# Second MLP in pairs of column chunks, with seven products of blocks in place of eight in some units

## Reference

```python
h2 = _rms_norm(x, norm2_g)
x = x + (jax.nn.silu(h2 @ w_gate) * (h2 @ w_up)) @ w_down   # w_gate, w_up: 2048 x 5632; w_down: 5632 x 2048
```

## Time and profile before

| | us |
|---|---|
| median of 3 runs | 2493.56 (2493.5 to 2493.63) |
| the profiled execution, its own time | 2493.6 |
| its span, first to last instruction | 2491.9 |
| TensorE busy in it | 2482.4 (100%) |
| VectorE busy | 1379.8 (55%) |
| ScalarE busy | 1120.3 (45%) |

### The profile page before, as it was taken

How to read it: one execution, slowest core, us unless ns; L and a number is a source line. 1 busy time by engine, 2 the same in 40 slices (tenths; PEclk the granted TensorE clock), 3 DMA queues, 4 the chain that set the end, 5 groups by cost and what they waited for, 6 DMA issues and landing times.

```text
span 2491.9 us, 28047 instructions
## 1 busy us (share of the span) xinstructions
PE 2482.4 (100%) x11885; PEld 2076.6 (83%) x11885; DVE 1379.8 (55%) x1129; ACT 1120.3 (45%) x1100; POOL 116.6 (5%) x95
## 2 busy tenths in 40 slices
PE   9999999999999999999999999999999999999999
PEld 8888888888888888888888888788888888888887
DVE  5675455454655555545555558876544444444444
ACT  5545533434444434334334457874533333333332
POOL 0410010010100000000000010000200000000000
PEclk9999999999999999999999999999999999999999
DMA  7555465666656565565555555444555665565554
GB/s 249 170 185 179 159 196 193 194 194 192 231 186 203 191 198 186 190 198 186 189 192 193 186 186 185 137 157 164 184 188 186 196 192 186 186 200 188 187 189 148
DMA packets 242731, 467.12 MB, mean 187 GB/s; under 512 B 11248, under 2 KB 22016, under 8 KB 242222
## 3 DMA queue, kind: packets, MB, share of 16 engines
q1 hardware_dynamic: 241054, 460.08, 56.9%
q10 hardware_dynamic: 1552, 5.25, 0.5%
HBM read 463.20 MB, written 2.10 MB: 187 GB/s over the span
## 4 chain that ended last, share of the span: by engine, by line
PE 96%; DVE 2%; ACT 1%; issue 1%; POOL 0%; DVEq 0%; ACTq 0%; POOLq 0%
PE acc L409 26%; PE acc L400 26%; PE acc L402 26%; PE acc L429 5%; PE acc L435 2%; PE tp L429 2%; PE sd L429 2%; PE sd L435 1%; PE tp L435 1%; PE tp L455 1%; PE sd L1338 1%; DVE wlo L385 1%; PE tp L1356 0%; PE sd L1347 0%; ACT whi L380 0%
## 5 line engine op out<-in xcount | busy, mean ns | idle before, releaser
L385 DVE TENSOR_TENSOR wlo<-raw,whi 128x2048 fp32r<-128x2048 f32 (+1 forms) x440 | 1014.6, 2307 | 957.8 <-ACT whi L380 957.2
L380 ACT ACTIVATE whi<-raw 128x2048 fp32r<-128x2048 f32 (+1 forms) x440 | 832.2, 1893 | 1067.5 <-PE acc L409 919.5
L400 PE MATMUL acc<-whi,opA_hi 128*128 128x512 f32 x1888 | 740.7, 392 | 0.1
L402 PE MATMUL acc<-whi,opA_lo 128*128 128x512 f32 x1888 | 735.1, 389 | 0.0
L409 PE MATMUL acc<-wlo,opA_hi 128*128 128x512 f32 x1888 | 469.2, 390 | 0.2 <-DVE wlo L385 0.2
L400 PE MATMUL acc<-whi,opB 128*128 128x512 f32 (+1 forms) x1088 | 422.3, 389 | 1.5 <-ACT whi L380 1.5
L402 PE MATMUL acc<-whi,opB 128*128 128x512 f32 (+1 forms) x1088 | 419.1, 386 | 0.0
L400 PEld LDWEIGHTS acc<-whi,opA_hi 128*128 128x128 f32 x1888 | 354.4, 188 | 74.0 <-issue 0.9
L402 PEld LDWEIGHTS acc<-whi,opA_lo 128*128 128x128 f32 x1888 | 354.6, 188 | 72.6
L409 PEld LDWEIGHTS acc<-wlo,opA_hi 128*128 128x128 f32 x1888 | 353.0, 188 | 73.4 <-DVE wlo L385 0.8
L409 PE MATMUL acc<-wlo,opB 128*128 128x512 f32 (+1 forms) x1088 | 266.4, 387 | 0.1
(11 more groups left out here) (308 smaller groups left out, 1297.8 us busy)
## 6 DMA issues: line engine op xcount, KB each, us to landing
raw<-in_w_in SPq DMA_DIRECT2D x116, 1024.0 KB, 5.5
raw<-in_w_mlp_up SPq DMA_DIRECT2D x64, 1024.0 KB, 5.3
raw<-in_w_mlp_down SPq DMA_DIRECT2D x64, 1024.0 KB, 5.0
raw<-in_w_gate SPq DMA_DIRECT2D x44, 1024.0 KB, 5.2
raw<-in_w_up SPq DMA_DIRECT2D x44, 1024.0 KB, 5.1
raw<-in_w_down SPq DMA_DIRECT2D x44, 1024.0 KB, 5.0
raw<-in_w_out SPq DMA_DIRECT2D x32, 1024.0 KB, 5.0
raw<-in_w_branch SPq DMA_DIRECT2D x16, 1024.0 KB, 5.0
```

The lines of the kernel that those rows point to most:

```text
L380: eng.activation(whi[:, j % SPL, k, 0:cols], raw[:, j, k, 0:cols], ACT.Copy).then_inc(hi_split, share(k))
L385: eng.tensor_tensor(wlo[:, j % SPL, k, 0:cols], raw[:, j, k, 0:cols], whi[:, j % SPL, k, 0:cols].bitcast(F32), ALU.subtract).then_inc(lo_s ...
L400: eng.matmul(acc[:, pair, m, 0:cols], hi[:, kt + i, m * P:(m + 1) * P], whi[:, s, i, 0:cols], start=first and i == 0, stop=False)
L402: eng.matmul(acc[:, pair, m, 0:cols], lo[:, kt + i, m * P:(m + 1) * P], whi[:, s, i, 0:cols], start=False, stop=False)
```

## The change

**Pairs.** A run now takes two column chunks at once and all four banks of `acc`. A gate pair is the gate and the up chunk of the same hidden channels: 8 units, each 2 channel tiles of both (`b` = 0 gate, `b` = 1 up). A down pair is two column chunks of down: 6 units in the first part, 8 in the others. The 132 units stay, in 11 gate pairs and 6 down pairs (gate x3, down x2, gate x4, down x2, gate x4, down x2). The load of a unit is two DMAs in place of one.

**Units of seven.** In units 3 and 5 of a pair (only 5 in the first gate pair, 3 and then 1 and 3 in the two down pairs of the first part) the 2 by 2 blocks (two token tiles, two channel tiles, two column chunks) are multiplied by seven products of blocks in place of eight, in Winograd's form of Strassen's algorithm: 21 matmuls in place of 24. That makes 21 such units in gate pairs and 11 in down pairs, 32 of the 132. Three products are summed straight into `acc`, the other four into `sd` and `tp`. VectorE makes four sums of weight blocks per unit (`t_sum`), ScalarE and VectorE split seven blocks of 512 columns in place of four (`seven_high`, `seven_low`). The sums of the activations' blocks are made four times (`operand_sums`): at unit 4 of the first gate pair, and at unit 6 of the last gate pair of each part. The four extra sums are put together behind the last unit of a pair (`combine`, with a copy `q_sum` by ScalarE) and added in as the banks are read.

**The pair's end.** The first and the last unit of a pair go bank by bank (6 matmuls each). All four banks are taken up again by the next pair, so TensorE waits for each bank before its first product in it (`bank_free`): for the SiLU in `acc[:, 0]` behind a gate pair, which itself waits for VectorE's add into the bank, and for VectorE's read elsewhere. VectorE reads the banks (`finish`) behind the split of the next pair's first unit.

```diff
+PAIR_UNITS = KT // 2
+GATE_SEVEN, DOWN_SEVEN = (3, 5), (3, 5)
...
+        PAIRS = []
+        unit, chunks2, seven2 = G_PAIR0 * UN, 0, 0
+        for part, size in enumerate((CH2_FIRST, CH2_LOOP, CH2_LOOP)):
+            for c in range(size):
+                PAIRS.append(Pair(len(PAIRS), "gate", unit, PAIR_UNITS, GATE_SEVEN if PAIRS else GATE_SEVEN[1:], 0,
+                                  GATE_SEVEN[0], (part, c), chunks2))
+                unit += PAIR_UNITS
...
+            for n in range(2):
+                seven = DOWN_SEVEN if part else (1, 3) if n else (3,)
+                PAIRS.append(Pair(len(PAIRS), "down", unit, size * CT // 2, seven, 1, DOWN_SEVEN[0] if part else 1,
+                                  (part, n), chunks2))
+                unit += size * CT // 2
...
+        A_SUMS = {(0, 4): 0}
+        for q in PAIRS:
+            if q.kind == "gate" and PAIRS[q.n + 1].kind == "down":
+                A_SUMS[q.n, 6] = 1
...
+            for p in PAIRS:
...
+                for v in range(p.units):
...
+                    sp.wait_ge(lo_split, (u - RAW + 1) * HV)
+                    to = raw[:, u % RAW].rearrange("p (a b) c -> p a b c", a=2)
+                    for b in range(2):
+                        if p.kind == "gate":
+                            src = (w_gate2, w_up2)[b][:, 2 * v:2 * v + 2, chunk(first + n)]
+                        else:
+                            src = w_dn2[:, first * CT + 2 * v:first * CT + 2 * v + 2, chunk(2 * n + b)]
+                        sp.dma_start(to[:, :, b, :], src).then_inc(landed[u % RAW], 16)
...
+            def seven_high(p, v):
...
+                if last_seven(p, v):
+                    act.wait_ge(units_used, last_seven(p, v))
+                act.activation(seven_hi[:, 0, :], raw[:, u % RAW, 0, :], ACT.Copy)
+                act.activation(seven_hi[:, 1:3, :], raw[:, u % RAW, 2:4, :], ACT.Copy).then_inc(hi_split, 1)
+                act.wait_ge(t_made, 3 * n + 1)
+                act.activation(seven_hi[:, 3:5, :], t_sum[:, 0:2, :], ACT.Copy)
+                act.wait_ge(t_made, 3 * n + 3)
+                act.activation(seven_hi[:, 5:7, :], t_sum[:, 2:4, :], ACT.Copy).then_inc(hi_split, 1)
+            def silu_gates(p):
...
+                act.wait_ge(hidden2, p.gates * MT)
+                for m in range(MT):
+                    act.wait_ge(bank_read, 4 * p.n + m + 1)
+                    act.activation(silu_gate[:, m, :], acc[:, 0, m, :], ACT.Silu, scale=rstd[:, m:m + 1]).then_inc(silu_in, 1)
+            for p in PAIRS:
+                for v in range(p.units):
+                    if v in p.seven:
+                        seven_high(p, v)
+                    else:
+                        hi_unit(act, (p.unit + v) // UN, (p.unit + v) % UN)
...
+                    if v == 0 and p.n and PAIRS[p.n - 1].kind == "gate":
+                        silu_gates(PAIRS[p.n - 1])
...
+                    if (p.n, v) in A_SUMS:
...
+                        act.wait_ge(a_made, n + 1)
+                        act.activation(a_hi[k][:, :, :, :], a_sum[:, :, :, :], ACT.Copy).then_inc(a_high, 1)
+                    if v == p.units - 1:
+                        act.wait_ge(units_used, p.unit + p.seven[-1] + 1)
...
+                        act.activation(q_sum[:, :], sd[:, 0, :], ACT.Copy).then_inc(q_copied, 1)
...
+            def bank_free(p, b, m):
+                if p.n == 0:
+                    pe.wait_ge(read_dve, readers_before(R_PAIR0 - 1 + b, "D") * MT)
+                elif PAIRS[p.n - 1].kind == "gate" and b == 0:
+                    pe.wait_ge(silu_in, PAIRS[p.n - 1].gates * MT + m + 1)
+                else:
+                    pe.wait_ge(bank_read, 4 * (p.n - 1) + 2 * b + m + 1)
+            def plain_products(p, v, hi, lo):
...
+                s, first, last = u % SPL, v == 0, v == p.units - 1
+                pe.wait_ge(hi_split, (u + 1) * HV)
+                def high(b, m, a):
...
+                    pe.matmul(acc[:, b, m, :], hi[:, 2 * v + a, rows], whi[:, s, 2 * a + b, :], start=first and a == 0, stop=False)
+                    pe.matmul(acc[:, b, m, :], lo[:, 2 * v + a, rows], whi[:, s, 2 * a + b, :], start=False, stop=False)
+                def low(b, m, a):
...
+                                     start=False, stop=last and a == 1)
+                banks = [(b, m) for b in range(2) for m in range(MT)]
+                if first or last:
+                    for b, m in banks:
+                        if first:
+                            bank_free(p, b, m)
+                        for a in range(2):
+                            high(b, m, a)
+                        pe.wait_ge(lo_split, (u + 1) * HV)
+                        for a in range(2):
+                            mm = low(b, m, a)
+                        if last and (b, m) != banks[-1]:
+                            mm.then_inc(bank_done, 1)
+                else:
+                    for a in range(2):
+                        for b, m in banks:
+                            high(b, m, a)
+                    pe.wait_ge(lo_split, (u + 1) * HV)
+                    for a in range(2):
+                        for b, m in banks:
+                            mm = low(b, m, a)
+                mm.then_inc(units_used, 1)
+            def seven_products(p, v, hi, lo):
...
+                k1, k2, up, down = 2 * v, 2 * v + 1, slice(0, P), slice(P, T)
+                sums = lambda i: (a_hi[p.op][:, i, x, :], a_lo[p.op][:, i, x, :])
+                own = [(sd[:, 0, :], (hi[:, k1, up], lo[:, k1, up]), 0, True),
+                       (acc[:, 0, 0, :], (hi[:, k2, up], lo[:, k2, up]), 1, False),
+                       (acc[:, 1, 0, :], sums(0), 2, False)]
+                made = [(sd[:, 1, :], sums(1), 3, True), (tp[:, 1, :], sums(2), 4, True), (tp[:, 0, :], sums(3), 5, True),
+                        (acc[:, 0, 1, :], (hi[:, k2, down], lo[:, k2, down]), 6, False)]
+                if first:
...
+                        pe.wait_ge(combined, p.combined)
+                        pe.wait_ge(q_copied, p.n)
...
+                    pe.wait_ge(a_low, sums_made(p))
+                for done, products in ((1, own), (2, made)):
+                    pe.wait_ge(hi_split, u * HV + done)
+                    for bank, (a_h, a_l), i, alone in products:
+                        pe.matmul(bank, a_h, seven_hi[:, i, :], start=alone and first, stop=False)
+                        pe.matmul(bank, a_l, seven_hi[:, i, :], start=False, stop=False)
+                    pe.wait_ge(lo_split, u * HV + done)
+                    for bank, (a_h, a_l), i, alone in products:
+                        mm = pe.matmul(bank, a_h, seven_lo[:, i, :], start=False, stop=alone and last)
+                mm.then_inc(units_used, 1)
+            for p in PAIRS:
+                hi, lo = (opB_hi, opB_lo) if p.op == 0 else (opA_hi, opA_lo)
+                for v in range(p.units):
...
+                    (seven_products if v in p.seven else plain_products)(p, v, hi, lo)
...
+                    if v == 0 and p.n and PAIRS[p.n - 1].kind == "gate":
+                        pe.wait_ge(hidden2, p.turned * MT)
+                        turn(pe, lambda m, b: stage[:, m, b * P:(b + 1) * P], T_HID2 + (p.turned - 1) * MT)
...
+            def seven_low(p, v):
...
+                if last_seven(p, v):
+                    dve.wait_ge(lo_split, last_seven(p, v) * HV)
+                dve.wait_ge(a_low, sums_made(p))
+                dve.tensor_tensor(t_sum[:, 0, :], w[:, 0, :], w[:, 1, :], ALU.add)
+                dve.tensor_tensor(t_sum[:, 1, :], w[:, 1, :], w[:, 3, :], ALU.add).then_inc(t_made, 1)
+                dve.wait_ge(t_made, 3 * n + 1)
+                dve.tensor_tensor(t_sum[:, 2, :], t_sum[:, 0, :], w[:, 3, :], ALU.add).then_inc(t_made, 1)
+                dve.wait_ge(t_made, 3 * n + 2)
+                dve.tensor_tensor(t_sum[:, 3, :], t_sum[:, 2, :], w[:, 2, :], ALU.add).then_inc(t_made, 1)
+                if last_seven(p, v):
+                    dve.wait_ge(units_used, last_seven(p, v))
+                dve.wait_ge(hi_split, u * HV + 1)
+                dve.tensor_tensor(seven_lo[:, 0, :], w[:, 0, :], seven_hi[:, 0, :].bitcast(F32), ALU.subtract)
+                dve.tensor_tensor(seven_lo[:, 1:3, :], w[:, 2:4, :], seven_hi[:, 1:3, :].bitcast(F32),
+                                  ALU.subtract).then_inc(lo_split, 1)
...
+                dve.tensor_tensor(seven_lo[:, 3:7, :], t_sum[:, :, :], seven_hi[:, 3:7, :].bitcast(F32),
+                                  ALU.subtract).then_inc(lo_split, 1)
+            def operand_sums(k, n, p):
...
+                own.done(dve.tensor_tensor(a_full[:, :, :, :], of(hi), of(lo), ALU.add))
...
+                own.mark(dve.tensor_tensor(a_sum[:, 1, :, :], a21, a22, ALU.subtract))
+                own.done(dve.tensor_tensor(a_sum[:, 2, :, :], a21, a11, ALU.subtract))
+                own.done(dve.tensor_tensor(a_sum[:, 3, :, :], a22, a_sum[:, 2, :, :], ALU.subtract))
```

(97 more changed lines are left out.)

198 lines of the change are left out of this document (79 added, 119 removed).

## The result

| | before | changed kernel |
|---|---|---|
| median, us | 2493.5 (7 runs, 2493.24 to 2493.63) | 2501.67 (7 runs, 2500.33 to 2503.89) |
| ratio | | 1.0033, 95% interval 1.0023 to 1.0042 |
| profiled execution: own time, span | 2493.6, 2491.9 | 2502.18, 2500.5 |

The changed kernel is 8.2 us slower, 0.33%. The forecast was 4.6 us slower, 2498.2; the time lies in the range, and the sign is the one that I gave the greater chance. The change itself is 1.8 times the one forecast: it is a small difference of two large sums.

A forecast was written before the change was run, and what follows sets the result against it. TensorE, busy throughout the second MLP, was taken to bound the kernel. 27.0 us of new waits against 22.4 saved made it 4.6 us slower, 2493.6 + 4.6 = 2498.2 us, range 2490 to 2509.

The forecast's parts named there:

- the sign: Whole kernel: slower was given 0.48, same 0.36, faster 0.16.
- The two sums: Second MLP: 22.4 us saved, mostly 96 fewer matmuls, against 27.0 us of new TensorE waits.
- rival A: Units of seven don't keep pace; 1 us over the slack in each gives 2530 us; chance 0.07.
- The ends of pairs: TensorE waits for banks behind pairs and for sums and a SiLU table load; 27.0 us in all.
- The down ends: Behind five down pairs, `combine` with three more adds to x makes TensorE 1.61 us late each; 8.1 us.
- the three ends with sums: Last gate pair of each part, `operand_sums` at unit 6: 3.4 us of lateness each, 10.3 us together.
- the first sums: First `operand_sums`, at unit 4 of the first pair, makes unit 5 wait 2.3 us.
- The regular gate end: Behind eight gate pairs, VectorE's add and the SiLU release TensorE 0.63 us late each; 5.0 us.
- The price of the write into a bank: VectorE's add into a bank behind gate pairs, taken as 0.69 us for 512 columns, between 0.60 and 1.23.
- rival C: Clock halves for a unit behind each of 13 idle stretches over 1.1 us: 71 us, 2569; chance 0.03.
- The tail: Kernel's very end: VectorE has one add behind the last matmul and not two, saving 0.6 us.
- Rival B: `operand_sums` hide behind unit 6, removing some 10.7 us of the waits: 2487.5 us; chance 0.13.

The follow-up runs named there:

- experiment 7: The changed kernel with the three moves of experiments 2, 3 and 4, down pairs' first bank read early, and adds to x a unit later; 2471.84 us.
- experiment 8: As experiment 7, but with 18 units of seven in place of 32; 2481.17 us.
- experiment 2: The changed kernel with the three adds of `combine` to x moved behind the bank reads, in all down pairs but the last; 2495.72 us.
- experiment 3: The changed kernel with the first `operand_sums` one unit earlier, the others at unit 1 of the down pair, their rounding and remainder a unit behind; 2491.73 us.
- experiment 4: The changed kernel with VectorE's add into a gate pair's first bank moved ahead of the next pair's split; 2491.9 us.
- experiment 5: The changed kernel with a two-column SiLU added at unit 6 of the first pair, so its table loads there; 2500.97 us.
- experiment 1: The changed kernel's pairs, loads and banks without units of seven, `operand_sums`, `combine` or adds into banks; 2492.82 us.
- experiment 6: The changed kernel with the moves of experiments 2, 3 and 4 together, and down pairs' first bank read early; 2473.12 us.

## Why the prediction was right, point by point

**The two sums** (what is saved, what the ends cost) were the right account. 96 matmuls went, and 21.8 us with them: experiment 7 shows it with all waits gone, experiment 8 unit by unit. That the units keep pace (rival A against it) is shown: no unit of seven has a wait but the one behind the first `operand_sums`, and experiment 8 leaves no cost for them.

**The ends of pairs.** All five kinds of wait came at their places and from the releasers named. The down ends (1.61, measured 1.66), the three ends with sums (10.3, 10.3) and the first sums (2.3, 2.3) were sized right; experiments 2 and 3 took each away by an edit that touched it alone, and the span fell by the measured size of the waits. The regular gate end was sized too low, 0.63 for 0.77. The price of the write into a bank was the one open, with bounds 0.60 and 1.23, and was right; VectorE's groups by shape have

```profile
L2423 DVE TENSOR_TENSOR acc<-acc,q_sum 128x512 f32<-128x512 f32 x11 | 7.6, 692 | 0.0
```

so the 0.7 us that "Perfetto Trace Analysis" of the Trainium skill would have added for PSUM isn't there. What the working lacked are some hundredths of a us at each hand-over. At the end at 1851.27 VectorE's add took from 1850.57 to 1851.26, ScalarE began at 1851.36, and TensorE's first matmul was at 1852.19: 1.62 from the start of the add, where I had 0.69 + 0.03 + 0.69 + 0.06 = 1.47 and 0.10 for the second matmul. Over the eight that is 1.1 of the 1.4 us by which the waits were undersized; the rest is in the down ends.

**The clock, rival C.** It had 0.03, as one mechanism with 71 us. It came in small. In the profiled execution the eleven of the 13 stretches that take up to 1.61 us left the clock at 1.00, among them eight of 1.56 to 1.61. The two of 1.99 and 2.19 were each followed by a fall in some executions; in all five profiled executions with a fall (the changed kernel, experiments 2 to 5) it stands right behind one of these two. The step that failed is "a clock of 1.00 throughout": a term of its own was due for the two gaps near 2 us, and a fall lasts for 3.4 us, with a cost of 1.6, where the rival had 5.44 for each.

The single times say the same. The changed kernel has 2500.33, 2500.55 and 2500.6 at a mean clock of 1.0, and 2501.67, 2501.93, 2502.18 and then 2503.89 at 0.999: three levels. Experiment 2 leaves both gaps and has three too (2494.2 to 2494.5; 2495.7 to 2495.9; 2497.6 to 2497.7). The third would be a fall behind both gaps. No execution of it was profiled, but in experiment 2 the mean clock reads 1.0, 0.999 and 0.998 on its three levels. Experiments 3, 4 and 5 leave one gap and have two levels (2489.9 to 2490.2 and 2491.7 to 2492.2 in experiment 3, of 11 runs 5 and 6); all on the lower have a mean clock of 1.0, all on the upper 0.999. Experiments 1, 6, 7 and 8 have no gap near 2 us; all their runs have a mean clock of 1.0 and lie on one level, within 0.8 us. The Trainium skill, "TensorE: Matmul & The Clock Gate", in the section on what is actually happening, says that idle time brings the throttle back; by these runs that is so, and one idle stretch of 2 us is enough in 17 of the 28 executions of experiments 3 to 5. Why in these and not in the others stays open.

**The tail** was mis-sized: 0.6 forecast, 0.1 measured. The step that failed is "VectorE now has one add behind the last matmul". I had counted `combine` of a down pair, 4.94 us, in front of every next pair's split, and not in front of the last reads, where it ends only 1.1 us ahead of the last matmul's start. Experiment 1, which has no `combine`, shows the 0.6 as forecast.

**Rival B** (the sums hide) did not happen in the changed kernel, and experiment 3 shows what it was worth: 10.4 us of span, where I had 10.7.

**Together:** 1.4 for the waits, 1.6 for the clock, 0.5 for the tail and 0.5 mostly in slower matmuls right behind the restarts are the 4.0 us by which the span of the profiled execution grew beyond the forecast. All four go the same way, so the forecast wasn't saved by errors that cancel; they also nearly doubled the change, and the range held it because it had been drawn wide for other causes, the write into a bank above all. The same account carried the version that beats both kernels, within 0.3 us of what was expected of it.

## What to carry to other kernels

When work goes from the bounding engine to its helpers, two sums decide: the instructions saved by their start-to-start distance, and the lateness at each hand-over, followed through the programs of the helpers in their order. Here 28.4 us of waits stood against 21.8 saved though no helper was over 79% busy, and moving a few instructions behind those that someone waits for, with the work unchanged, turned 8.2 us slower into 21.6 faster. A repair must be followed to the next hand-over too: each of experiments 2 and 4 left a small new wait at a place that the old one had covered.

## What the hardware showed that I had not expected

- Idle stretches of TensorE of 1.36 to 1.64 us left its granted clock at 1.00 in every profiled execution. Of the executions with one stretch of 1.99 or 2.19 us, 17 of 28 show a fall by their time and mean clock. In the five profiled ones with a fall the clock was at 0.50 for 3.4 us, from 0.1 to 1.3 us after the engine had started again. One fall costs 1.6 us in the trace, and a kernel's single times lie on levels 1.4 to 2.0 apart.
- Out of idle time the second matmul starts 0.30 to 0.34 us behind the first, where 0.227 is usual (1790.28 and 1790.62; 1933.36 and 1933.66).
- VectorE's add with its result in a bank takes 692 ns for 512 columns, the same as into SBUF (693 in the earlier trace rows).
